# Projections of a block turned from tiles of weights as the stationary operand to tiles of tokens, with the short convolution's taps read from PSUM

## The reference, cut to what matters

```
hn = rmsnorm(x, norm1_w)
proj = hn @ w_in                              # 2048 -> 7184 of its 11280 columns are meant here
conv_out = centred_depthwise_conv(proj[..., :5120], conv_w, conv_b)   # 3 taps over the tokens
hv, hx1, hx2 = conv_out[..., :3072] split in three of 1024    # the Hyena branch: FFT-like long convolutions
q, k = silu(conv_out[..., 3072:5120])         # the mLSTM branch
v, o = proj[..., 5120:6144], sigmoid(proj[..., 6144:7168])
g = proj[..., 7168:7184] + mlstm_gate_bias    # 16 gate columns
```

## Time and profile before

| what | value |
|---|---|
| median of three runs | 2752.8 us (2751.95 to 2752.91) |
| the profiled execution's own time | 2751.39 us |
| its span | 2749.4 us |
| granted TensorE clock, mean of the span | 0.994 |
| PE busy | 2696.6 us, 98% |
| DVE / ACT / POOL busy | 41% / 45% / 43% |
| DMA | 489.00 MB, mean 178 GB/s |

### The profile page before, as it was taken

One profiled execution on the slowest core, in us unless ns is written; L12 is line 12 of the kernel. 1 busy time (PEld: TensorE's weight loads), 2 busy tenths in 40 slices (PEclk: granted clock), 3 DMA queues, 4 the chain that ended last, 5 costly groups with the idle time before them and its releaser, 6 DMA issues.

```text
span 2749.4 us, 33936 instructions
## 1 busy us (share of the span) xinstructions
PE 2696.6 (98%) x13886; PEld 2295.9 (84%) x13886; DVE 1129.0 (41%) x1347; ACT 1229.5 (45%) x1512; POOL 1183.8 (43%) x536
## 2 busy tenths in 40 slices
PE   9999999999999999999999989999999999999999
PEld 8998877778888888888888878988788888888887
DVE  6777754433432222222333376636432222222222
ACT  6434444444444444444444445445454444444333
POOL 3555653344444444444444345422244444444443
PEclk9999999999999999999999999999999999999999
DMA  6444434355555555555555534443355555555554
GB/s 236 161 158 158 159 138 176 138 199 184 187 188 190 188 192 189 186 194 186 192 203 190 196 136 141 170 168 123 127 183 194 186 186 197 185 197 185 203 196 152
DMA packets 73161, 489.00 MB, mean 178 GB/s; under 512 B 8443, under 2 KB 10140, under 8 KB 15536
## 3 DMA queue, kind: packets, MB, share of 16 engines
q1 hardware_dynamic: 73008, 486.84, 50.4%
HBM read 484.71 MB, written 2.10 MB: 177 GB/s over the span
## 4 chain that ended last, share of the span: by engine, by line
PE 88%; DVE 5%; ACT 2%; issue 2%; POOL 1%; DMA 1%; SPq 0%; DVEq 0%; ACTq 0%; POOLq 0%
PE PB L578 24%; PE PB L582 24%; PE PB L579 24%; PE PB L550 3%; PE PB L546 3%; PE PB L547 3%; PE PB L596 1%; ACT WH L1109 1%; DVE WL L1649 1%; DMA RAW<-in_w_in_a 1%; POOL WL L2454 1%; PE PB L697 1%; DVE TM L2353 1%; PE PB L675 0%; PE PB L766 0%
## 5 line engine op out<-in xcount | busy, mean ns | idle before, releaser
L2454 POOL TENSOR_TENSOR WL<-RAW,WH 128x1024 fp32r<-128x1024 f32 x442 | 1074.8, 2432 | 1456.4 <-ACT WH L1109 1456.4
L1109 ACT ACTIVATE WH<-RAW 128x1024 fp32r<-128x1024 f32 x892 | 940.1, 1058 | 1183.2 <-PE PB L582 1091.2
L1649 DVE TENSOR_TENSOR WL<-RAW,WH 128x1024 fp32r<-128x1024 f32 x450 | 583.7, 1298 | 1452.1 <-ACT WH L1109 1451.8
L578 PE MATMUL PB<-WH,HNH 128*128 128x512 f32 x1888 | 742.6, 393 | 7.2 <-DVE MIX L2292 4.6
L582 PE MATMUL PB<-WL,HNH 128*128 128x512 f32 x1888 | 736.5, 390 | 7.5 <-POOL WL L2454 4.5
L579 PE MATMUL PB<-WH,HNL 128*128 128x512 f32 x1888 | 735.6, 390 | 0.0
L578 PEld LDWEIGHTS PB<-WH,HNH 128*128 128x128 f32 x1888 | 355.1, 188 | 85.9 <-DVE MIX L2292 5.8
L582 PEld LDWEIGHTS PB<-WL,HNH 128*128 128x128 f32 x1888 | 354.9, 188 | 84.0 <-POOL WL L2454 5.9
L579 PEld LDWEIGHTS PB<-WH,HNL 128*128 128x128 f32 x1888 | 355.1, 188 | 72.2
L546 PE MATMUL PB<-HNH,WH 128*128 128x256 f32 x1184 | 345.2, 292 | 3.1 <-ACT WH L1109 3.0
L550 PE MATMUL PB<-HNH,WL 128*128 128x256 f32 x1184 | 338.7, 286 | 7.4 <-POOL WL L2454 5.1
(11 more groups left out here) (347 smaller groups left out, 2074.9 us busy)
## 6 DMA issues: line engine op xcount, KB each, us to landing
RAW<-in_w_gu SPq DMA_DIRECT2D x176, 1024.0 KB, 4.8
RAW<-in_w_dn SPq DMA_DIRECT2D x88, 1024.0 KB, 4.8
RAW<-in_w_in_a SPq DMA_DIRECT2D x56, 1024.0 KB, 4.8
RAW<-in_w_in SPq DMA_DIRECT2D x45, 1024.0 KB, 4.8
RAW<-in_w_out SPq DMA_DIRECT2D x32, 1024.0 KB, 4.8
RAW<-in_w_ga SPq DMA_DIRECT2D x24, 1024.0 KB, 4.8
RAW<-in_w_gb SPq DMA_DIRECT2D x24, 1024.0 KB, 4.8
WIN<-in_win SPq DMA_DIRECT2D x8, 512.0 KB, 5.3
```

The costliest lines, as they stand in the source:

```text
L578: e.matmul(o, hi[:, k, x], WH[:, s, c], start=k == 0, stop=False)
L1109: e.activation(WH[:, u % NSPL, :], RAW[:, n % NRAW, half * SU * 128:(half + 1) * SU * 128], ACT.Copy).then_inc(*wt.act.mark(("wh", u)))
L1649: e.tensor_tensor(WL[:, u % NSPL, :], RAW[:, n % NRAW, half * SU * 128:(half + 1) * SU * 128], f32(WH[:, u % NSPL, :]), ALU.subtract).then ...
L2454: e.tensor_tensor(WL[:, u % NSPL, :], RAW[:, n % NRAW, half * SU * 128:(half + 1) * SU * 128], f32(WH[:, u % NSPL, :]), ALU.subtract).then ...
```

## The change

The 40 convolved rows become ten groups (tokens as rows): `group` with 512 columns each, in the same stream of weights. Their path through the other engines is new. At the end of a group ACT scales both halves from PSUM into SBUF with the norm's factor by token (`projected`, line 1440 of the changed kernel). In the next group's second quarter (tile 16) TensorE turns them with 8 transposes into two PSUM banks (`turn_projected`); at tiles 18 and 20 ACT takes the middle tap from PSUM for four channel tiles, and at tiles 20 and 22 DVE adds the outer taps, with the shifted operand in PSUM and the sum in SBUF. DVE's scaling of each row is gone. The silus come at tiles 26 and 28.

The gate row leaves the weight stream (57 blocks become 56, the head has 896 tiles instead of 912). Its 16 columns, padded to 32, are a small load WG (256 KB), and TensorE makes them in group 9 with 32 float32 matmuls in which four groups of 32 array columns take k-tiles 4q to 4q + 3; the four partial sums are added by the matmuls that already move the gates for the mLSTM branch.

At the start, the first two k-tiles of x and the first unit come in two pieces each, with high and low halves made by piece; later blocks of weights are issued between the pieces of x. Because a group needs four k-tiles for each 16 tiles, ACT and DVE normalise k-tiles 4 to 15 at tiles 1, 5, 9, ... of the first group, and the squares are spread over tiles 8 to 38.

```diff
-        for name, n in (("a", 24), ("qk", 16), ("g", 1), ("vt", 4), ("o", 4), ...
+        for name, n in (("a", 20), ("vt", 4), ("o", 4), ...
...
-            for i in range(8):
+            for k in range(2):
+                x, r = ("x0", "x8")[k], slice(512 * k, 512 * k + 512)
+                e.dma_start(XT[:, k, :], A["xT"][:, k, :]).then_inc(landed[x], 16)
+                e.dma_start(RAW[:, 0, r], A["w_in_a"][0][:, r]).then_inc(landed[f"raw{k}"], 16)
+            for i in range(1, 8):
                 e.dma_start(XT[:, 2 * i:2 * i + 2, :], A["xT"][:, 2 * i:2 * i + 2, :]).then_inc(landed[f"x{i}"], 16)
-                if i == 3:
+                if i == 1:
                     e.dma_start(RAW[:, 0, half:2 * half], A["w_in_a"][0][:, half:2 * half]).then_inc(raw_landed[0], 16)
-            raw(1)
-            raw(2)
+                if i in (3, 5):
+                    raw(i // 2)
...
+            e.dma_start(WG[:, :, :], A["w_g"]).then_inc(landed["wg"], 16)
             raw(3)
...
+            def gates():
+                b = wide_bank("g")
+                e.wait_ge(landed["wg"], 16)
+                for q in range(4):
+                    for x in (HNH, HNL):
+                        for c in range(4):
+                            k = 4 * q + c
+                            t = e.matmul(b[32 * c:32 * c + 32, 0:T], WG[:, k, :], f32(x[:, k, :]),
+                                         start=q == 0 and x is HNH, stop=q == 3 and x is HNL, tile_position=(0, 32 * c))
...
-            for j in range(24):
-                ...
-                    tile_row(j, 16, hn_ready(0) if j == 0 else None)
...
+            for g in range(14):
+                hooks, banks = {}, None
+                if 1 <= g < 11:
+                    hooks[1] = lambda: turn_projected(g - 1)
+                if g == 0:
+                    banks = [wide_bank("a", 0), wide_bank("a", 1)]
+                    hooks[3] = first_sums
+                elif g == 1:
+                    hooks[0] = lambda: rstd_turned(0)
+                elif g == 9:
+                    hooks[2] = gates
+                group(NT["a"] + 2 * g, HNH, HNL, 16, None if g else hn_ready(0), hooks, banks)
...
+            def projected(g):
+                for h in range(2):
+                    e.wait_ge(*wt.pe.done("nt", nt))
+                    ...
+                    e.activation(SIG[:, h, :], (mb(nt) if g else bank("a", h))[:, 0:512], ACT.Copy, scale=RTOK[:, h:h + 1])
+            def conv_middle(g, q):
+                e.wait_ge(*m.pe.done("pr", g, q))
+                for i in range(2):
+                    e.activation(conv_to(j), bank("pr", g, q)[:, 256 * i:256 * i + 256], ACT.Identity, bias=vec("cb", j),
+                                 scale=vec("cw1", j))
+            for g in range(10):
+                for k in tiles(64):
+                    if g == 0:
+                        if k % 4 == 1 and k < 48:
+                            first_normed(4 + k // 4)
+                        if k % 2 == 0 and 8 <= k < 40:
+                            square(0, i // 2, i % 2, XT[:, i, :])
+                        if k == 52:
+                            root_mean(0)
+                    else:
+                        short_conv(g - 1, k)
+                projected(g)
...
+            def conv_outer(g, q):
+                b, js = bank("pr", g, q), [4 * g + 2 * q, 4 * g + 2 * q + 1]
+                e.wait_ge(*m.act.done("cm", js[1]))
+                for i, j in enumerate(js):
+                    e.scalar_tensor_tensor(out=y[:, 1:T], in0=b[:, 256 * i:256 * i + T - 1], scalar=vec("cw0", j),
+                                           in1=y[:, 1:T], op0=ALU.mult, op1=ALU.add)
...
```

More of the change, by code:

```diff
@@ L302, in build @@
         STAT = ar("STAT", [128, 3, 4, 4], 47.5)
-        order = [("w_in_a", i) for i in range(57)]
+        order = [("w_in_a", i) for i in range(56)]
         order += [("w_ga", i) for i in range(24)] + [("w_gb", i) for i in range(24)]
@@ L470, in sync @@
             w.beside(w.side, 1.12)
-            run(33 * 16)
+            run(32 * 16)
             w.rest()
@@ L960, in tensor @@
             w.beside(hyena(), 1.04, 7)
-            for j in range(24):
[L962 to L965, removed]
-                    tile_row(j, 16, hn_ready(0) if j == 0 else None)
[L967 to L975, removed]
+            for g in range(14):
+                if g == 6:
+                    w.beside(w.side, 1.12)
+                hooks, banks = {}, None
[9 more added lines that the diff above has]
+                group(NT["a"] + 2 * g, HNH, HNL, 16, None if g else hn_ready(0), hooks, banks)
             w.rest()
@@ new lines, in vector @@
+            normed(0, 2, "norm1", XT[:, 2, :])
+            normed(0, 3, "norm1", XT[:, 3, :])
+            low(1)
+            w.beside(hyena(), 1.04, 7)
+            for g in range(10):
+                if g == 6:
+                    w.beside(w.side, 1.12)
+                for k in tiles(64):
+                    if g == 0:
+                        if k % 4 == 2 and k < 48:
+                            normed(0, 4 + k // 4, "norm1", XT[:, 4 + k // 4, :])
+                        if k % 4 == 3 and 12 <= k < 40:
+                            add_square(0, k // 4 - 2)
+                        if k == 54:
+                            inverted(0)
+                    elif k in (20, 22):
+                        conv_outer(g - 1, (k - 20) // 2)
+                    if g == 9 and k == 38:
+                        e.wait_ge(*m.pe.done("g"))
+                        e.tensor_tensor(G16[:, :], bank("g")[:, 0:T], RSTD[:, :], ALU.mult).then_inc(*m.dve.mark(frees("g")))
+                        e.wait_ge(*m.dve.prev())
+                        e.tensor_scalar(G16[:, :], G16[:, :], vec("gbias"), None, ALU.add).then_inc(*m.dve.mark("g"))
+                if g == 0:
+                    token_scale(0)
@@ L2240, in vector @@
+            for k in tiles(16 * 16):
+                if k in (20, 22):
+                    conv_outer(9, (k - 20) // 2)
             w.rest()
@@ L2553, in gpsimd @@
             w.beside(hyena(), 1.04, 7)
-            for j in range(24):
-                for k in tiles(16):
-                    if j == 1 and k % 2 == 0 and k > 1:
-                        add_square(0, k // 2)
+            for k in tiles(24 * 16):
+                if k % 4 == 1 and 12 <= k < 40:
+                    add_square(0, k // 4 - 2)
             w.beside(w.side, 1.12)
@@ L2694 @@
     w = one["w_in"]
-    a["w_in_a"] = np.concatenate([units(np.concatenate([tiles(w[:, 0:5120]), tiles(padded(w[:, 7168:7184]))])),
-                                  groups(w[:, 5120:7168])])
+    a["w_in_a"] = groups(w[:, 0:7168])
+    a["w_g"] = np.ascontiguousarray(padded(w[:, 7168:7184], 32).reshape(16, 128, 32).transpose(1, 0, 2))
     a["w_ga"] = groups(w[:, 7184:9232], one["w_branch_a"])
@@ L2754 @@
     put("b2", one["filt_b2"].reshape(64, 1))
+    put("gsum", np.tile(np.eye(32, 16, dtype=np.float32), (4, 1)))
     put("gbias", one["mlstm_gate_bias"].reshape(16, 1))
```

184 lines of the change are left out of this document (81 added, 103 removed).

## The result

| what | before | changed |
|---|---|---|
| median of five runs each | 2752.91 us (2751.95 to 2753.97) | 2767.84 us (2763.06 to 2769.18) |
| ratio, 95% interval | | 1.0048 (1.0033 to 1.0063) |
| profiled execution's own time, span | 2751.39, 2749.4 us | 2769.18, 2765.9 us |
| granted clock, mean | 0.994 | 0.995 |
| PE / DVE / ACT / POOL busy | 98 / 41 / 45 / 43% | 98 / 38 / 45 / 42% |

The account below looks back on a forecast made before the run. The kernel was taken as a stream of TensorE matmuls with few holes (PE busy 98%). Terms -12.5 + 10.0 + 1.4 + 5.7 - 4.9 = -0.3 us on the median 2752.8 gave 2752.5 us, range 2738 to 2763.

Parts of the forecast that it names:

- Behind the end of the head: After 423.7 us, instructions and their places in the walk were said to stay the same; costed at nothing.
- the bound of 0.2%: A difference under 0.2%, 5.5 us, was held to be hardly distinguishable from none in measuring this kernel.
- signs of being right: Listed trace checks: starts 0.227 apart, turns of 1.0 us, two early waits, group 1 from 40 to 43 us, long waits' places.
- Matmuls: In the head, ten groups of 512 columns replace 40 rows of 256, half as many matmuls: -12.5 us.
- Turns: Eight transposes per group on TensorE's path, 1.0 us for each of ten turns: +10.0 us.
- Rival 4: The turns pull the clock down, 1.7 us lost for each of ten, +17: 2769.5 us; chance 0.03.
- Gates: The gate row's 5.8 us becomes 32 float32 matmuls, two at a time, 7.2 us: +1.4, between -2.2 and +8.6.
- Rival 3: Column groups do not overlap: gates take 14.4 us, 7.2 more, giving 2759.7 us; chance 0.10.
- The start: First group: TensorE waits for k-tile 10 behind unit 6, then for the squares: +5.7 us, from +1.7 to +8.
- Waits beside Hyena: Idle time and slow clock in the head's later windows fall from 19.7 to 14.8 us: -4.9, between -14 and +9.
- Rival 2: DVE's burst of eight taps holds up WL in five of eight places, +4.3 instead of -4.9: 2761.7 us; chance 0.18.
- rival 1: DVE's relief is worth more than its burst costs, waits -13.7 instead of -4.9: 2743.7 us; chance 0.33.

Follow-up runs that it names:

- e2: The kernel before with 64 unused bytes behind the small vectors (VEC), nothing else changed: 2774.5 us, ratio 1.0073.
- e3: The kernel before with 32 unused bytes behind the small vectors (VEC), nothing else changed: 2772.8 us, ratio 1.0068.
- e4: The kernel before with 128 unused bytes behind the small vectors (VEC), nothing else changed: 2772.1 us, ratio 1.0064.
- e7: The kernel before with 64 unused bytes just ahead of the arena, so that only the arena moves: 2771.9 us, ratio 1.0073.
- e5: The changed kernel with gsum in a free part of the arena, loaded by its own DMA, so every tile keeps its old place: 2741.9 us, ratio 0.9958.
- e12: e5 with all 32 gate matmuls on one column group, one sum instead of four: 2753.9 us, ratio 0.9998 to the kernel before.
- e11: e5 with the first loads of the kernel before (x in eight pieces, first unit in one): 2743.6 us, ratio 0.9964 to the kernel before.
- e8: e5 with k-tiles 4 to 15 normalised at every second tile instead of every fourth: 2745.8 us, ratio 0.9975 to the kernel before.
- e9: e8 with the norm's sum, root and factor moved into group 1, group 0 turned a quarter later: 2740.3 us, ratio 0.9949 to the kernel before.
- e10: The kernel before with WH and WL 64 bytes off and all behind them moved by 256: 2764.3 us, ratio 1.0035.
- e6: The kernel before with 256 unused bytes behind the small vectors (VEC): 2755.8 us, ratio 1.0008.

## Why the prediction was wrong, point by point

**The step that failed** is the one in a half sentence: "Behind the end of the head ... the instructions and their places in the walk stay the same ..., and I cost all of it at nothing." The instructions did stay; their operands' addresses did not. The prediction's part on the change never looked at VEC's size. The step cost +21.6 us in 85% of the span, four times the bound of 0.2%, by a mechanism that no rival held. e2, e3, e4 and e7 make the loss in the kernel before, e5 takes it away from the changed one. The prediction's signs of being right nearly all came true (starts, turns, both early waits, group 1 at 42.7 us, the places of the long waits), and its time was still outside the range: no sign looked at the stretch behind the head.

**The head** was forecast at -0.3 us and gave -5.1 (with e5 -6.9). Term by term:

- *Matmuls, -12.5*: right. Groups of the head run at the 0.227 of the earlier trace rows; their stationary operand is HNH or HNL, ahead of VEC.
- *Turns, +10.0*: nearly right. From the first transpose to the matmul behind them it is 0.79 us in nine turns and 0.85 in the one shown, and with the slower next start 0.9, some 9 in all:

```profile
74.10 1.09 PE L604 MATMUL PB<-IDENT,TM 128*128 128x128 f32 x8
74.95 0.48 PE L586 MATMUL PB<-WH,HNH 128*128 128x512 f32 x1
75.27 0.40 PE L587 MATMUL PB<-WH,HNL 128*128 128x512 f32 x1
```

  The granted clock was 1.00 over the whole stretch of nine turns (the window 42.70 to 302.40 above). Rival 4 is out: of the rule in the Trainium skill (TensorE: Matmul & The Clock Gate, Part 4) that it drew on, no effect is seen with turns this short.
- *Gates, +1.4*: mis-sized. 3.5 us against the row's 5.8 is -2.3, the lower end. The reasoning that a matmul's second record must wait for its first, so that two run at a time, is refuted by the 0.44 us of e5 against the 1.73 of e12. Nor is 0.45 us for one, read off a record whose end is modelled, quite right: by the starts it is 0.43 (e12). The trace agrees with the Trainium skill (TensorEngine Tiling (Array Packing), Theoretical Speedup) here: a factor of 4.0 (12.1 us against 3.05 for seven steps) of the up to four that it promises. Rival 3 is out; e12 shows what it would have cost, 10.2 us on e5's head (group 10 at 311.9 us instead of 301.7).
- *The start, +5.7*: right in its mechanism and nearly in size. TensorE's two waits stand where the prediction put them, the second behind POOL's sum of squares rather than DVE's:

```profile
30.49 0.58 PE L586 MATMUL PB<-WH,HNH 128*128 128x512 f32 x1 [2.79 <-issue]
35.47 1.22 PE L644 MATMUL PB<-SQA,ONES 128*128 128x256 f32 x4 [0.27 <-POOL SQA L2519]
```

  The chain of waits there begins with the DMA, as forecast:

```profile
15.53 11.66 DMA RAW<-in_w_in_a
...
27.21 1.06 ACT WH L1132
28.27 0.32 ACT SQT L1160
...
34.59 0.74 POOL SQA L2519
```

  WH of unit 6 starts at 27.21 (forecast 27.0), group 1 at 42.7 (41.8): +6.6. The granted clock was 0.50 from 30.8 to 34.1 us, behind the first of the two waits, which the middle of the forecast did not have; in e5 it was 1.00 there, and group 1 began at 42.3. e11 bears out that the finer loads bring next to nothing, e8 and e9 that k-tile 10 and the squares are two limits, both of which must go.
- *Waits beside Hyena, -4.9*: the places were right, in groups 3, 6 and 10 and at the last inverse; the sizes were not.

```profile
121.33 0.50 PE L590 MATMUL PB<-WL,HNH 128*128 128x512 f32 x1 [1.32 <-POOL WL L2501]
...
206.84 0.50 PE L590 MATMUL PB<-WL,HNH 128*128 128x512 f32 x1 [1.32 <-POOL WL L2501]
...
326.75 0.50 PE L590 MATMUL PB<-WL,HNH 128*128 128x512 f32 x1 [1.31 <-POOL WL L2501]
...
400.41 1.83 PE L720 MATMUL PB<-DG,UP 128*128 128x128 f32 x7 [3.29 <-POOL UP L2549]
```

  1.3, 1.3, 1.3 and 3.3 us stand against 2.4, 2.4, 0.6 and 2.8. The small waits are 3.0 us instead of 1.5, one of them for the new work of ACT, which the prediction had beside the matmuls: TensorE waits 1.4 us at 70.6 us for `projected`, with which ACT comes late. Idle time in all is 10.2 us (forecast 9.7, before 12.9). The forecast also had a slow clock behind three of the waits. Only the last is followed by one: 0.50 from 399.40 to 406.20 us. From group 1 on, the head lasts 375.9 us against 386.4. Of these -10.5, matmuls are -11.3 (the first group has 1.2 of the 12.5), turns +9, gates -2.3; left for waits and clock are -5.9, and -7.3 in e5. By the windows 2.7 of that is idle time, in both; the rest goes with the clock, which from group 1 on is at 0.50 once instead of four times. Rival 2 is out: it had five waits of 2.8 us, and there are three of 1.3 and one of 3.3. Taps from PSUM take the time forecast, 480 ns:

```profile
L1753 DVE SCALAR_TENSOR_TENSOR X<-PB,VEC,X 128x255 f32<-128x255 f32 x16 | 6.9, 472 | 4.3 <-ACT X L1453 4.3
L1758 DVE SCALAR_TENSOR_TENSOR X<-PB,VEC,X 128x255 f32<-128x255 f32 x16 | 6.9, 471 | 0.0
```

Together, as differences from the forecast: gates -3.7, turns -1, waits -1.0 (what the other terms leave), start +0.9, in sum the -4.8 between the head's -5.1 and the -0.3. Without the shift, rival 1 (2743.7, or 2740 with a better start) is nearest to e5's 2741.9, but its mechanism is only half of that: the waits for POOL's WL shrank and did not go, more of the gain is clock than waiting time, and the gates gave 2.3 us. That its number is the nearest is in part luck.

The medians of e5 and before are 11.0 us apart and their profiled executions 7.1. The one profiled of e5 was its slowest of five, the one of before among its fastest, and no more is to be read from the difference.

## What to carry to other kernels

A diff that resizes one small tile moves all that is laid out behind it: before costing the untouched part of a kernel at nothing, write down the start addresses of the operands of its commonest instruction, of both kernels. A table that grows goes at the end of the layout, or is padded so that what lies behind it keeps its place; and where a span grows while instructions, idle time and clock stay the same, compare one shape's mean time by operand name, which shows in two rows what no list of waits can. Where an operand lies can cost or gain, by the shape: e10 made groups slower and rows faster, and only the starts by shape showed it, not the time. At the start of a kernel, the removal of one wait pays only with the next limit: here k-tile 10 and the sum of squares had to be moved together.

## What the runs showed of the hardware that was not expected

- A float32 matmul of a group (512 moving columns, halves rounded to fp32r) costs 226.8 ns at full clock when its stationary operand lies on the grid of the kernel before, and 233.3 when it is 32 or 64 bytes off; 128 bytes off costs about the same, 256 nothing (e2, e3, e4, e6, e7).
- The moving operand 64 bytes off costs 0 to 4 ns of the same matmul, 2.0 on average. A row's matmul (256 moving columns) with its stationary operand 64 bytes off is faster, 115.9 ns instead of 119.9 (e10).
- Two-record float32 matmuls on four column groups run four at once: 0.44 us for four, 1.73 on one column group (e5, e12).
- Waits of 1.3 us left the granted clock at 1.00 in the changed kernel, one of 3.3 us was followed by a stretch at 0.50. The same wait is not always followed by one: behind the wait of 2.8 us for k-tile 10 the clock was 0.50 in the changed kernel and 1.00 in e5, whose wait was 2.5.

Left open: what in the memory or in the loading of weights makes the place count; why rows gain where groups lose; why 128 bytes off is a shade better than 64; whether the costs of the two operands add up (no run moved both off their grid); and whether e9's gain over e5 of 3.7 us at the end of the head holds in its time.
